# The first expert's step taken out of the loop, with three of its weight units in the place of the first mixer's weight ring

## The reference, cut to what matters

```python
def moe(h, router_w, router_b, w_up, b_up, w_down, b_down):
    logits = xt @ router_w + router_b
    top_vals, top_idx = lax.top_k(logits, TOP_K)        # TOP_K 4 of 32 experts
    gates = jax.nn.softmax(top_vals, axis=-1)
...
    hcat = xblk @ w_up[e] + b_up[e]                      # w_up[e]: 1024 x 2048
    x_glu = jnp.minimum(hcat[:, 0::2], SWIGLU_LIMIT)
    x_lin = jnp.clip(hcat[:, 1::2], -SWIGLU_LIMIT, SWIGLU_LIMIT)
    act = x_glu * jax.nn.sigmoid(SWIGLU_ALPHA * x_glu) * (x_lin + 1.0)
    return act @ w_down[e] + b_down[e]                   # w_down[e]: 1024 x 1024
```

## Time and profile before

| | us |
|---|---|
| median of 3 runs | 1803.07 (1800.07 to 1805.18) |
| the profiled execution's own time | 1801.11 |
| its span | 1799.3 |
| TensorE matmul busy | 1736.2 (96%) |
| VectorE busy | 686.3 (38%) |
| ScalarE busy | 598.3 (33%) |
| GpSimd busy | 65.5 (4%) |
| mean granted clock of TensorE | 0.984 of full speed |

### The profile page before, as it was taken

One profiled execution on the slowest core, in us unless ns is written; L12 is line 12 of the kernel. 1 busy time (PEld: TensorE's weight loads), 2 busy tenths in 40 slices (PEclk: granted clock), 3 DMA queues, 4 the chain that ended last, 5 costly groups with the idle time before them and its releaser, 6 DMA issues.

```text
span 1799.3 us, 25946 instructions
## 1 busy us (share of the span) xinstructions
PE 1736.2 (96%) x10761; PEld 1177.0 (65%) x10761; DVE 686.3 (38%) x1161; ACT 598.3 (33%) x815; POOL 65.5 (4%) x50
## 2 busy tenths in 40 slices
PE   6989989999999999999999999999999999999998
PEld 6989864444443434444343434448999999989996
DVE  3568651112121212212121212124498555557654
ACT  3734421111111111111111111124465578555434
POOL 2003100000000000000000000000020011100000
PEclk9989988999999999999999999998999999999999
DMA  8443376999999999999999999984555444455552
GB/s 252 141 141 118 117 303 259 431 427 431 429 431 429 433 428 430 430 431 431 427 432 429 431 429 433 427 339 125 181 185 165 141 141 136 149 178 182 186 184 97
DMA packets 150276, 534.92 MB, mean 297 GB/s; under 512 B 5524, under 2 KB 103956, under 8 KB 117457
## 3 DMA queue, kind: packets, MB, share of 16 engines
q1 hardware_dynamic: 148976, 531.06, 74.8%
q0 software_dynamic: 1248, 3.14, 0.5%
HBM read 533.13 MB, written 1.05 MB: 297 GB/s over the span
## 4 chain that ended last, share of the span: by engine, by line
PE 69%; DMA 13%; ACT 1%; DVE 1%; issue 0%; SPq 0%; DVEq 0%; ACTq 0%
PE bank L1156 20%; DMA expert_weights<-in_expert_w_up_dram 13%; PE bank L123 9%; PE bank L124 9%; PE bank L125 9%; PE bank L1172 9%; PE bank L1134 5%; PE bank L1146 3%; PE bank L1163 2%; PE bank L1654 0%; PE bank L1140 0%; PE bank L1681 0%; PE bank L1688 0%; PE bank L1670 0%; ACT back_w_hi L107 0%
## 5 line engine op out<-in xcount | busy, mean ns | idle before, releaser
L1156 PE MATMUL bank<-expert_weights,x_gathered 128*64 128x512 f32 x1536 | 338.6, 595 | 2.9 <-DMA expert_weights<-in_expert_w_up_dram 2.9
L1156 PEld LDWEIGHTS bank<-expert_weights,x_gathered 128*64 128x64 f32 x1536 | 106.7, 137 | 212.0 <-issue 200.3
L111 DVE TENSOR_TENSOR back_w_lo<-raw_weights,back_w_hi 128x2048 fp32r<-128x2048 f32 x90 | 206.3, 2294 | 96.5 <-ACT back_w_hi L107 95.5
L1172 PE MATMUL bank<-expert_weights_late,activations 128*64 128x512 f32 x1024 | 226.8, 595 | 0.0
L107 ACT ACTIVATE back_w_hi<-raw_weights 128x2048 fp32r<-128x2048 f32 x90 | 170.1, 1891 | 100.3 <-PE bank L125 100.3
L123 PE MATMUL bank<-u_hi,back_w_hi 128*128 128x256 f32 x704 | 201.7, 287 | 0.2 <-DVE u_lo L1478 0.2
L124 PE MATMUL bank<-u_lo,back_w_hi 128*128 128x256 f32 x704 | 199.8, 284 | 0.0
L125 PE MATMUL bank<-u_hi,back_w_lo 128*128 128x256 f32 x704 | 199.7, 284 | 0.0
L1071 DVE COPY step_cols<-expert_slots 128x2 f32 (+1 forms) x33 | 5.6, 169 | 438.1 <-PE bank L1140 438.1
L1098 DVE TENSOR_TENSOR pre_act<-bank,bias_now 128x512 f32<-128x512 f32 x64 | 44.0, 687 | 315.9 <-PE bank L1163 315.9
L1172 PEld LDWEIGHTS bank<-expert_weights_late,activations 128*64 128x64 f32 x1024 | 70.7, 137 | 130.1 <-issue 127.9
(11 more groups left out here) (375 smaller groups left out, 2627.0 us busy)
## 6 DMA issues: line engine op xcount, KB each, us to landing
expert_weights<-in_expert_w_up_dram SPq DMA_DIRECT2D x96, 2048.0 KB, 19.8
expert_weights_late<-in_expert_w_down_dram SPq DMA_DIRECT2D x64, 2048.0 KB, 18.0
raw_weights<-in_expert_w_up_dram SPq DMA_DIRECT2D x32, 2048.0 KB, 19.9
raw_weights<-in_w_in_dram SPq DMA_DIRECT2D x62, 1024.0 KB, 5.3
raw_weights<-in_w_up_dram SPq DMA_DIRECT2D x22, 1024.0 KB, 5.1
raw_weights<-in_w_down_dram SPq DMA_DIRECT2D x10, 1024.0 KB, 5.0
raw_weights<-in_w_s_out_dram SPq DMA_DIRECT2D x8, 1024.0 KB, 5.0
raw_weights<-in_w_out_dram SPq DMA_DIRECT2D x4, 1024.0 KB, 5.0
```

The lines of the kernel that those rows point to most:

```text
L111: dve.tensor_tensor(self.w_lo[:, s, 0:size], self.s.raw[:, s, 0:size], self.w_hi[:, s, 0:size].bitcast(FP32), ALU.subtract).then_inc(self. ...
L1156: m = pe.matmul(U[b][rows[half], :], lhsT=xg[:, 2 * u + a, :], rhs=w[:, a, 512 * c:512 * c + 512], start=(first and a == 0), stop=(last an ...
L1172: m = pe.matmul(U[0][rows[c], :], lhsT=act_t[:, b, g, half, :], rhs=w[:, half, g, 512 * c:512 * c + 512], start=(b + half + g == 0), stop= ...
```

## The change

It gives the step of expert 0 code of its own, ahead of the loop, on TensorE and SP (ScalarE and VectorE keep their loops from 0). Units 0, 1 and 2 of expert 0 go to a new place, `expert_weights_extra`, which lies over the first mixer's two weight rings, and units 0, 1 and 2 of expert 1 are loaded into the normal places at the end of the mixer. The new place is free after the first step, and `ln2_params` (8 KB of each partition) goes there; so POOL's two loads of it wait for `unit_mm` to reach 6.

```diff
@@ mixer1, sync
                 sp.wait_ge(hg_done, 4)
-                for u in (1, 2, 3):
-                    s.load_expert_unit(sp, u, 0)
+                s.load_expert_unit(sp, 3, 0)
+                for u in (1, 2):
+                    s.load_expert_unit(sp, u, 1)
                 sp.wait_ge(st.gemm_done, NW + 8)
                 s.load_expert_unit(sp, 4, 0)
                 sp.wait_ge(st.lo_done, N_UNITS - 1)
-                s.load_expert_unit(sp, 0, 0)
+                s.load_expert_unit(sp, 0, 1)
                 sp.wait_ge(st.gemm_done, NW + 12)
+                for u in range(EXTRA):
+                    s.load_expert_unit(sp, u, 0, s.extra[:, u, :], s.extra_full[u])
                 s.load_expert_unit(sp, 5, 0)
@@ experts
         sb("late_units_place", [P, 2, KD * 512])
+        sb("extra_units_place", [P, EXTRA, KD * 512])
+        extra = s.extra
...
-        ln_gb = sb("ln2_params", [P, 2, D])
+        ln_gb = extra[:, 0, 0:2 * D].rearrange("p (a d) -> p a d", a=2)
...
             s.load_first(sp, 2)
             n = n_steps(sp)
-            with sp.Fori(0, n - 1) as i:
+            for u in range(EXTRA, UNITS):
+                sp.wait_ge(unit_mm, u + 1)
+                load(sp, u, 1)
+            with sp.Fori(1, n - 1) as i:
                 for u in range(UNITS):
                     sp.wait_ge(unit_mm, i * UNITS + u + 1)
                     load(sp, u, (i + 1) % N_EXPERTS)
...
         def gpsimd(pool):
+            pool.wait_ge(unit_mm, UNITS)
             pool.dma_start(ln_gb[:, 0, :], A["ln2_g"][0].partition_broadcast(P)).then_inc(ln_loaded, 16)
             pool.dma_start(ln_gb[:, 1, :], A["ln2_b"][0].partition_broadcast(P)).then_inc(ln_loaded, 16)
...
+            def unit_loaded(u, i):
+                if u >= EXTRA:
+                    pe.wait_ge(full[u], (i + 1) * 16)
+                elif isinstance(i, int) and i == 0:
+                    pe.wait_ge(s.extra_full[u], 16)
+                else:
+                    pe.wait_ge(full[u], i * 16)
+
+            def unit_of(u, i):
+                return extra[:, u, :] if u < EXTRA and isinstance(i, int) and i == 0 else weights[u]
...
-            with pe.Fori(0, n) as i:
+            def step(i):
                 pe.wait_ge(gather_out, i + 1)
-                pe.wait_ge(full[0], (i + 1) * 16)
-                up_part(0, 1, True, False)
+                unit_loaded(0, i)
+                up_part(unit_of(0, i), 0, 1, True, False)
...
+            step(0)
+            with pe.Fori(1, n) as i:
+                step(i)
@@ whole_block
+        s.extra_full = [nc.alloc_semaphore(f"extra_unit{u}_full") for u in range(EXTRA)]
...
-            with nc.sbuf_tensor("expert_weights_late", [P, 2, KD * 512], FP32) as late:
+            with nc.sbuf_tensor("expert_weights_late", [P, 2, KD * 512], FP32) as late, \
+                    nc.sbuf_tensor("expert_weights_extra", [P, EXTRA, KD * 512], FP32) as s.extra:
```

More of the change, by code:

```diff
@@ L28 @@
 N_EXPERTS, TOP_K, SLOTS = 32, 4, 64
-EXPERT_UNITS = 6
+EXPERT_UNITS, EXTRA = 6, 3
 PASSES = T // SLOTS
@@ L1148, in scatter_rows, with up_part @@
                 return m
-            def up_part(u, b, first, last):
-                w = weights[u].rearrange("p (a n) -> p a n", a=2)
+            def up_part(w, u, b, first, last):
+                w = w.rearrange("p (a n) -> p a n", a=2)
                 for a in range(2):
@@ L1178, in tensor @@
             n = n_steps(pe)
-            with pe.Fori(0, n) as i:
+            def unit_loaded(u, i):
[8 more added lines that the diff above has]
+            def step(i):
                 pe.wait_ge(gather_out, i + 1)
-                pe.wait_ge(full[0], (i + 1) * 16)
-                up_part(0, 1, True, False)
+                unit_loaded(0, i)
+                up_part(unit_of(0, i), 0, 1, True, False)
                 pe.wait_ge(y_out, i + 1)
-                up_part(0, 0, True, False).then_inc(unit_mm, 1)
+                up_part(unit_of(0, i), 0, 0, True, False).then_inc(unit_mm, 1)
                 for t in range(TT):
@@ L1188, in tensor @@
                 for u in range(1, 3):
[L1189 to L1194, removed]
+                    unit_loaded(u, i)
+                    up_part(unit_of(u, i), u, 0, False, False)
+                    up_part(unit_of(u, i), u, 1, False, False).then_inc(unit_mm, 1)
+                unit_loaded(3, i)
+                up_part(unit_of(3, i), 3, 0, False, True).then_inc(first_mm, 1)
+                up_part(unit_of(3, i), 3, 1, False, True).then_inc(unit_mm, 1)
                 pe.wait_ge(up_out, i * 2 + 1)
@@ L1202, in tensor @@
                 for b in range(2):
-                    pe.wait_ge(full[4 + b], (i + 1) * 16)
+                    unit_loaded(4 + b, i)
                     pe.wait_ge(act_ready, i * 2 + b + 1)
                     down_part(b)
+            step(0)
+            with pe.Fori(1, n) as i:
+                step(i)
             pe.wait_ge(y_out, n + 1)
@@ L2004, in whole_block, with load_expert_unit @@
         s.raw_full = {name: [nc.alloc_semaphore(f"{name}_raw_full{i}") for i in range(RING)] for name in ("m1", "back")}
+        s.extra_full = [nc.alloc_semaphore(f"extra_unit{u}_full") for u in range(EXTRA)]
         s.expert_full = [nc.alloc_semaphore(f"expert_unit{u}_full") for u in range(EXPERT_UNITS)]
-        def load_expert_unit(sp, u, e):
+        def load_expert_unit(sp, u, e, place=None, full=None):
+            place, full = (s.expert_units[u], s.expert_full[u]) if place is None else (place, full)
             if u < 4:
                 w = A["expert_w_up"][0].rearrange("e (u p a) n -> e u p (a n)", p=P, a=2)[bass.ds(e, 1), u, :, :]
-                sp.dma_start(s.expert_units[u], w.rearrange("o p n -> (o p) n")).then_inc(s.expert_full[u], 16)
+                sp.dma_start(place, w.rearrange("o p n -> (o p) n")).then_inc(full, 16)
             else:
                 w = A["expert_w_down"][0].rearrange("e (c p g) n -> e p c (g n)", p=P, g=2)[bass.ds(e, 1), :, 2 * (u - 4):2 * (u - 4) + 2, :]
-                sp.dma_start(s.expert_units[u].rearrange("p (c n) -> p c n", c=2), w.rearrange("o p c n -> (o p) c n")).then_inc(s.expert_full[u], 16)
+                sp.dma_start(place.rearrange("p (c n) -> p c n", c=2), w.rearrange("o p c n -> (o p) c n")).then_inc(full, 16)
         s.load_expert_unit = load_expert_unit
```

## The result

The changed kernel takes 1807.42 us (median of 6 runs, 1804.49 to 1808.74) against 1803.02 us (6 runs): a ratio of 1.0022, with a 95% interval of 1.0012 to 1.0032. That is 4.4 us longer by the medians, and, under 0.3%, what the prediction calls the same. The two profiled executions, 1804.88 us and 1801.11 us, lie 3.8 us apart.

A forecast was written before the change was run, and what follows sets the result against it. The loop's end was taken as the DMA restart at 310.75 us plus all DMA work behind it. Terms 0 + 0 + 3.2 + 0 = 3.2 us longer, on 1803.1 us, gave 1806.3 us, called "the same"; range 1801 to 1811 us.

The forecast's parts named there:

- What bounds the loop: Experts' loop: TensorE needs 28.70 us a step, DMA engines 29.24 us; DMA sets the end once the lead is gone.
- ceiling: End of the experts' loop: weights that are never late would be worth 4.9 us, and no more.
- the restart: SP's issue of expert 1's unit 4 at 310.75 us; from there the DMA engines are full to the loop's end.
- The change-over: Experts' loop: the chain first shows unit 3's transfer at about 765 us (710 to 790 us), instead of 933 us.
- The three extra units: Expert 1's units 0 to 2, loaded before the loop: they end before an idle gap; gain 0, at most 0.2 us.
- POOL's wait: POOL's ln2 and queued loads move from 274.26 to 314 us, adding 1.21 MB behind the restart: 3.2 us (2.8 to 4.6).
- Fetch ahead: At 247.08 us SP issues expert 0's units 0 to 2, then unit 5; done by 273.9 us, in time: cost 0.
- step 0's code: Step 0 outside the loop, TensorE's loop entry moving from 283 to 314 us: cost 0, up to 0.3 us.
- A: Experts' loop: the lead counts, so TensorE sets the pace to step 31; 4.9 us shorter, 1798.2 us; chance 8%.
- B: At 314 to about 323 us POOL's loads disturb the weight stream; price 5.2 to 6.6 us, 1809.1 us at 6; chance 14%.
- C: Edge between mixer and experts' programs: start delayed by draining weights, 1.2 us on top of 3.2, 1807.5 us; chance 10%.
- D: Behind the restart: POOL's late loads are free, filling holes the DMA share does not show; 1803.1 us; chance 8%.

The follow-up runs named there:

- e7: Kernel before, only half of unit 5 brought in the loop: stretch (unit 4's issue in step 0 to turn behind last unit 3) 880.47 us, ratio 0.9967.
- e8: Kernel before with the nine places kept as a refilled ring, ln2_params in its own place, POOL not waiting: stretch 880.62 us, ratio 0.9969.
- e1: Changed kernel with POOL waiting for unit_mm 1 (unit 0 only) instead of 6: stretch 884.97 us, ratio to the kernel before 1.0001.
- e3: Changed kernel with ln2_params in a place of its own and POOL not waiting: stretch 884.93 us, ratio to the kernel before 0.9995.
- e2: Kernel before with only POOL's wait for unit_mm 6 added: stretch 890.02 us, ratio to the kernel before 1.0028.
- e9: Ring-of-nine kernel with POOL's wait for unit_mm 6 put back: stretch 880.62 us, ratio to the kernel before 0.9968.
- e4: Changed kernel with w_dt, dt_bias and a_log issued ahead of POOL's wait, only ln2 loads late: stretch 888.08 us, ratio to the kernel before 1.0021.
- e5: Changed kernel with the two ln2 loads issued twice behind POOL's wait: stretch 891.42 us, ratio to the kernel before 1.0027.
- e10: Kernel before profiled once more, unchanged: stretch 885.72 us, against 885.36 us in its first profile.
- e12: Second profile of the kernel before with only POOL's wait for unit_mm 6 added: stretch 890.45 us.

## Why the prediction was right, and where it was not

*What bounds the loop* held in each number: two periods 0.54 us apart, a ceiling of 4.9 us (e7 measured 4.9 us, e8 came within 0.15 us of it), the end set by the restart plus the work behind it. The change-over came where it was forecast, "about 765 us", at 761.29 us and in the second profile at 760.25 us. That is in part luck: it follows the net of two wrong sizes (below), and it is coarse, since the kernel before has it at 933 us in one profile and at 902 us in the other. The forecast's own terms give 330 + 15 x 28.70 = 761 us, and for the bounds 4.6 and 2.8 us they give 686 and 782 us, not 710 and 790.

*The three extra units: gain 0, at most 0.2 us.* The mechanism, that these units end in front of a hole and so give no lead, is right: not 14.6 us, nor the 4.9 us that a lasting lead brings. The size is 0.6 us in e1 and e3, and 1.3 us beside the late loads (e2 against the changed kernel). The reading of the share 0.17 right after 311.0 us as "nothing left" stands: 0.16 MB, 0.4 us at 430 GB/s, was still to come when unit 4 was issued, but it was through before unit 4's first bytes, and the stream behind is no earlier without it (e3). So the 0.6 us has no cause that a run shows. Beside the late loads the bytes explain a part: without the leftover e2's kernel has moved 364.2 MB in 850 us, the changed one 364.35 MB, 0.15 MB or 0.35 us of the 1.3 us. The rest is open.

*POOL's wait: 3.2 us, bounds 2.8 to 4.6 us.* The mechanism was right and is shown by e1, e2 and e9 together: undone it vanishes, alone it brings the whole loss, and off the bound it is free. The size was too small: 4.0 us in the changed kernel (888.93 - 884.95), 4.7 us on the kernel before, just over the upper bound. The term that was mis-sized is what the loads cost beyond their bytes, taken as 3.2 - 2.8 = 0.4 us. The bytes show it: in the first 850 us of the stretch the changed kernel moved

```profile
DMA packets 32753, 364.33 MB, mean 429 GB/s; under 512 B 2846, under 2 KB 2878, under 8 KB 3166
```

with POOL's 1.21 MB among them, e1 364.81 MB without. So 0.48 + 1.21 = 1.69 MB of weights are missing, 3.9 us at 430 GB/s: 2.8 us are POOL's bytes, 1.1 us is stream that was lost, and it was lost close behind the restart: after 30 us the changed kernel is at 11.60 MB with POOL's bytes, e1 at 12.27 MB without, no less behind than at 850 us. By experiment: the small loads cost 0.85 us for 0.4 us of bytes (e4), and the first 1.05 MB 888.08 - 884.95 = 3.1 us, where a further 1.05 MB cost its bytes, 2.5 us (e5). The upper bound from busy shares, 3.6 to 4.6 us, came nearer, though the window that it was read from includes ramp and tail on idle engines; why the loss arises no run separates.

*Fetch ahead and step 0's code: 0 each.* Right. e3 has both and is not slower, and the fetch ahead was through at about 274 us, as forecast. The loop's entry behind step 0 is not quite free: from the issue of unit 4 to that of the next unit 0 SP takes 317.92 - 310.83 = 7.09 us, against 317.68 - 310.75 = 6.93 us before, and the repeats agree to 0.01 us. These 0.16 us are within the 0.3 us allowed, and the lead covers them.

The two wrong sizes nearly cancel: 4.0 - 0.6 = 3.4 us between the mean stretches (888.93 - 885.54), against 3.2 us forecast. That the sum is so near is luck. The medians' 4.4 us are another microsecond more; their 95% interval, 2.2 to 5.8 us, holds both. The forecast of 1806.3 us is 1.1 us short of the measured 1807.42 us.

*The rivals.* A, the lead counts: did not happen, but e8 shows what it would have taken, places that stay in use. The Trainium skill, "DMA: Bandwidth & Descriptors", section "Rules for kernel authors", says to issue early and wait late, and names the fixed setup cost as what overlaps. The prediction read it of the whole transfer; so read, it is right where something covers the transfer: e8 shows it. Here the same bytes early, at 274 or 289 us, were free and at 314 us were not. B, a disturbance of 5.2 to 6.6 us: out by size and by e5, though a part of it is real, the 1.1 us of stream lost behind the restart. C, a delay at the edge between the programs: VectorE's first work there follows TensorE's last by 1.25 us, as it did by 1.24 us, beside DMA engines that are now busy (share 0.72 in between, against 0.00):

```profile
269.26 3.69 PE L972 MATMUL bank<-b_down,gate_t 32*128 32x512 f32 x8 [0.46 <-ACT gate_t L495]
```

```profile
274.20 0.27 DVE L1094 MEMSET scatter<- 128x256 f32 x1 [3.44 <-PEq L975]
```

From 265 to 274.3 us neither trace has a packet in the instruction queues; both have one, 0.02 MB, behind it, by 276 us. By the Trainium skill, "Runtime: NRT & Kernel Launch", section "Instruction fetch mechanics", a taken branch out of the fetched window would need one; this trace shows neither the fetch nor its cost at this edge. D, free loads: out.

## What to carry to other kernels

When a transfer stream sets the end of a loop, a fetch ahead is worth only what it takes out of the stream behind the last idle gap; extra places that are filled once and dropped give a gap, and the same places kept as a ring give a lead, which lasts for a certain number of steps. Any load, however far from the critical path its reader is, costs at least about its bytes where the stream is full and sets the end: before adding a wait, look at the DMA share at the moment to which the load moves, and at the loads queued behind it. And ask for the earliest release that is enough: here unit 0 instead of unit 5 made the difference of the whole change.

## What the runs showed that was not expected

The stretch began at 307.9 to 313.4 us in the 14 profiles, though no kernel alters what lies before 226 us. In the window 120 to 160 us the granted clock was 0.91 in the first profile of the kernel before and 1.00 in the second profile of e2's kernel, windows of these two:

```profile
120.00:160.00 40.00, 36.94 (x291) 36.76 (x290) 25.45 (x29) 13.87 (x13) 4.81 (x2) 0.91 0.33 106
```

```profile
120.00:160.00 40.00, 36.67 (x310) 36.29 (x309) 28.13 (x32) 17.21 (x16) 5.69 (x3) 1.00 0.39 127
```

With the higher clock TensorE did 310 matmuls there instead of 291. In both TensorE waits 3.06 us for ScalarE at the same place (L876); behind it the windows of 4 us show the clock at 0.51 and 0.63, the lower of its two levels for most of the time, in the one execution, and at 1.00 in the other. Why it falls in some executions and not in others stays open. Four profiles have 1.00 in the window 120 to 160 us (e3, e8, e10, e12), and in these the stretch begins at 307.9 to 308.8 us; the ten others have 0.90 to 0.96 and begin at 309.8 to 313.4 us. So the clock there goes with the scatter, though it does not explain all of it. What follows the stretch varies too, from 603.2 to 605.7 us to the end of the span. With 5.5 us ahead of it the scatter is larger than the price in question, 4.0 us, and that is why a stretch inside the profile told more than medians of ten runs.
